# An encoder's front on one core: constant products from the beginning, another order of quarters and casts, a third weight tile, other homes for squares

## The reference, cut to what matters

```
mod = silu(c) @ w_mod + b_mod                     # per sequence: shift1, scale1, gate1, shift2, scale2, gate2
h   = rms_norm(x, g_mix) * (1 + scale1) + shift1  # norm over the 1024 features of a token
z   = h @ w_in                                    # 1024 x 1536: u_f | u_r | u_g
y_f = fourier_mixer(u_f)                          # FFT over sequence and head, real part, a small map per head
u_c = depthwise_conv(u_r)                         # 4 taps along the sequence
y_r = bidirectional_rglru(u_c) * gelu(u_g)        # gates from small products, linear recurrences both ways
x   = x + gate1 * (concat(y_f, y_r) @ w_out)
x   = x + gate2 * (square(relu(h2 @ w_ff1)) @ w_ff2)   # h2: second norm, width 4096 inside
y   = rms_norm(x, g_final)
```

## Time and profile before

| | us |
|---|---|
| median of 3 runs | 1403.32 (1403.24 to 1403.36) |
| profiled execution | 1403.55 |
| its span | 1401.8 |
| TensorE busy | 1379.7 |
| VectorE, ScalarE, GpSimd busy | 812.8, 588.1, 478.0 |

### The profile page before, as it was taken

How to read it: one execution, slowest core, us unless ns; L and a number is a source line. 1 busy time by engine, 2 the same in 40 slices (tenths; PEclk the granted TensorE clock), 3 DMA queues, 4 the chain that set the end, 5 groups by cost and what they waited for, 6 DMA issues and landing times.

```text
span 1401.8 us, 18026 instructions
## 1 busy us (share of the span) xinstructions
PE 1379.7 (98%) x7332; PEld 1170.7 (84%) x7332; DVE 812.8 (58%) x781; ACT 588.1 (42%) x703; POOL 478.0 (34%) x269
## 2 busy tenths in 40 slices
PE   5999999999999999999999999999999999999998
PEld 3877778898888888888888888888888888888887
DVE  5967688795438974555334453353746434354584
ACT  5667888665325632332222222342322223423152
POOL 0002111145003775574554545531432222333131
PEclk9999999999999999999999999999999999999999
DMA  9444411106210343343433334479997444445552
GB/s 368 170 158 158 155 63 38 46 31 215 116 61 31 120 162 124 137 146 140 152 122 114 127 141 152 166 276 388 377 388 285 151 150 155 167 173 197 200 189 90
DMA packets 75699, 231.27 MB, mean 165 GB/s; under 512 B 5729, under 2 KB 9953, under 8 KB 66786
## 3 DMA queue, kind: packets, MB, share of 16 engines
q1 hardware_dynamic: 75074, 229.60, 44.6%
q10 hardware_dynamic: 544, 0.52, 0.1%
HBM read 165.09 MB, written 65.01 MB: 164 GB/s over the span
## 4 chain that ended last, share of the span: by engine, by line
PE 95%; DVE 2%; DMA 1%; SPq 1%; issue 1%; ACT 0%; POOL 0%; DVEq 0%; ACTq 0%
PE bank L827 19%; PE bank L828 19%; PE bank L829 19%; PE bank L821 9%; PE bank L822 9%; PE bank L823 9%; PE bank L837 5%; PE bank L838 3%; DMA mod_first<-in_w_mod 1%; PE bank L866 1%; PE bank L878 0%; DVE two_r L2194 0%; SPq L590 0%; DVE n_t L2166 0%; PE bank L848 0%
## 5 line engine op out<-in xcount | busy, mean ns | idle before, releaser
L2585 POOL TENSOR_TENSOR w_lo<-w_raw,w_hi 128x2048 fp32r<-128x2048 f32 x28 | 134.7, 4812 | 319.6 <-ACT w_hi L1644 318.1
L2312 DVE TENSOR_TENSOR hin_two<-hin,hin_two 128x3072 fp32r<-128x3072 f32 x28 | 130.3, 4657 | 187.7 <-ACT hin_two L1656 187.7
L827 PE MATMUL bank<-hin_two,w_lo 128*128 128x512 f32 (+1 forms) x576 | 211.4, 367 | 0.0
L828 PE MATMUL bank<-hin_two,w_hi 128*128 128x512 f32 (+1 forms) x576 | 210.8, 366 | 0.0
L829 PE MATMUL bank<-hin_two,w_hi 128*128 128x512 f32 (+1 forms) x576 | 210.5, 365 | 0.0
L1644 ACT ACTIVATE w_hi<-w_raw 128x2048 fp32r<-128x2048 f32 x28 | 53.6, 1915 | 247.3 <-PE bank L838 150.2
L2577 POOL TENSOR_TENSOR w_lo<-w_raw,w_hi 128x512 fp32r<-128x512 f32 x43 | 65.4, 1520 | 183.8 <-ACT w_hi L1582 183.7
L827 PEld LDWEIGHTS bank<-hin_two,w_lo 128*128 128x128 f32 x576 | 108.6, 189 | 18.2 <-issue 0.2
L829 PEld LDWEIGHTS bank<-hin_two,w_hi 128*128 128x128 f32 x576 | 108.6, 189 | 17.7
L828 PEld LDWEIGHTS bank<-hin_two,w_hi 128*128 128x128 f32 x576 | 108.7, 189 | 17.0 <-issue 0.2
L1592 ACT ACTIVATE hid<-bank 128x768 f32<-128x768 f32 (+2 forms) x68 | 52.5, 773 | 162.8 <-PE bank L829 152.6
(11 more groups left out here) (297 smaller groups left out, 3473.5 us busy)
## 6 DMA issues: line engine op xcount, KB each, us to landing
hin<-hid_all SPq DMA_DIRECT2D x28, 1536.0 KB, 6.6
hid_all<-hid SPq DMA_DIRECT2D x105, 384.0 KB, 2.5
w_raw<-in_w_ff SPq DMA_DIRECT2D x36, 1024.0 KB, 9.1
mod_raw<-in_w_mod SPq DMA_DIRECT2D x16, 1024.0 KB, 6.0
w_raw<-in_w_ff SPq DMA_DIRECT2D x60, 256.0 KB, 3.2
x<-in_xT SPq DMA_DIRECT2D x5, 2048.0 KB, 14.3
w_sums<-w_raw SPq DMA_DIRECT2D x8, 1024.0 KB, 15.6
w_raw<-w_sums SPq DMA_DIRECT2D x8, 1024.0 KB, 9.7
```

Of the source, the lines that this page charges most:

```text
L827: pe.matmul(out, w_lo, v_hi, start=first, stop=False, skip_group_check=True)
L828: pe.matmul(out, w_hi, v_lo, start=False, stop=False, skip_group_check=True)
L2312: dve.tensor_tensor(hin_part(n % 3, LO), hin[n % 3][:].rearrange("p t n -> p (t n)"), hin_part(n % 3, HI), ALU.subtract).then_inc(hin_lo_d ...
L2585: pool.tensor_tensor(w2_lo[n % 2][:].rearrange("p t n -> p (t n)"), w2_raw[m % RAWS][:].rearrange("p t n -> p (t n)"), w2_hi[n % 2][:].rea ...
```

## The change

- TensorE: instead of 7 products of constants behind `norm_sum(1)`, 44 at the very beginning, ahead of `norm_sum(0)`.
- TensorE: `mod_quarter_sum(0)` comes right behind `mod_quarter(0)`. `front` takes a list of tiles; chunk 0 takes tiles 0, 1 and 2, in pieces; mod_quarter(3) and its sum move between other pieces. Product n = 6 (tile 2, chunk 0) is thereby part of the front; the banks, the order of the copies out (`FRONT`) and `in_tile`'s waits follow.
- ScalarE and VectorE: the row and columns of quarter 0 and the copy of rstd come ahead of the casts of tiles 0 and 1; these come between the first scalings and lo parts. Tile 2 is cast in the front, its lo part on VectorE and no longer on GpSimd.
- Tile 2 has a raw place of its own (`win_raw2`) and is loaded behind quarter 1, ahead of quarter 2.
- Each square has a home of its own, in three sets; chunk 2's lie in chunk 0's x and in the raw place of tile 2, and wait for those to be used up.
- The seven semaphores `op_lo[i]` become one that counts.

```diff
--- before
+++ after
@@ -230,6 +230,7 @@
     win_raw1 = place("win_raw1", [P, KD * P], F32, s2 + 4096)
+    win_raw2 = place("win_raw2", [P, KD * P], F32, W0 + 14336)
@@ -238,8 +239,9 @@
-    sq8 = place("sq8", [P, KD, CH], F32, W0)
-    sq8_other = place("sq8_other", [P, KD, CH], F32, A0 + 32768)
+    sq_at = ([A0 + 81920 + 2048 * k for k in range(KD)], [A0 + 32768 + 2048 * k for k in range(KD)],
+             [X0 + 2048 * k for k in range(4)] + [W0, W0 + 2048, W0 + 4096, W0 + 14336])
+    sq_tile = [[place(f"sq{n}_{k}", [P, CH], F32, o) for k, o in enumerate(homes)] for n, homes in enumerate(sq_at)]
@@ -406,6 +408,7 @@
     ld_x0 = sem("ld_x0_rest")
+    ld_win2 = sem("ld_win2")
@@ -464,7 +467,7 @@
     op_hi = sem("op_hi")
-    op_lo = [sem(f"op_lo{i}") for i in range(7)]
+    op_lo = sem("op_lo")
@@ -507,10 +510,6 @@
-    def squares(n):
-        return sq8_other if n == 1 else sq8
@@ -542,12 +541,16 @@
+    FRONT = (0, 3, 6, 1, 4, 2, 5)
...
     def in_bank(n):
-        return bank[(0, 1, 2, 3, 5, 4)[n] if n < 2 * NCH else n % 4]
+        return bank[(0, 3, 4, 1, 5, 7)[n] if n < 2 * NCH else n % 4]
     def in_order(n):
-        j, c = divmod(n, NCH)
-        return 2 * c + j + 1 if j < 2 else n + 1
+        return FRONT.index(n) + 1 if n in FRONT else n + 1
...
+    def raw_of(j):
+        return {1: win_raw1, 2: win_raw2}.get(j, win_raw)
@@ -601,12 +604,11 @@
         load_first(1)
+        sp.dma_start(win_raw2[:], w_in_d[TILES[2]]).then_inc(ld_win2, 16)
...
         sp.dma_start(dft_head[:], dft_head_d).then_inc(ld_dft, 16)
-        sp.wait_ge(win_lo_done, 1)
-        sp.dma_start(win_raw[:], w_in_d[TILES[2]]).then_inc(ld_win, 16)
@@ -843,7 +845,7 @@
                 pe.wait_ge(xn_done, xn_count(n))
-            total = squares(n)[:, 0, :] if shared(n) else n_acc[:]
+            total = sq_tile[n][0][:] if shared(n) else n_acc[:]
@@ -888,14 +890,13 @@
-        def front(c, q):
+        def front(c, q, tiles=(0, 1)):
             i = part_at[c, q]
-            for j in range(2):
+            for j in tiles:
...
                     pe.wait_ge(win_lo_done, j + 1)
-                    if j == 1:
-                        pe.wait_ge(rstd_copied, c + 1)
+                    pe.wait_ge(rstd_copied, c + 1)
@@ -913,7 +914,7 @@
             n = NCH * j + c
-            pe.wait_ge(in_evac, n - 3)
+            pe.wait_ge(in_evac, {2 * NCH + 1: 2, 2 * NCH + 2: 1, 3 * NCH: 4}.get(n, n - 3))
@@ -935,37 +936,42 @@
         pe.wait_ge(const_set, 4)
+        for b in range(44):
+            pe.matmul(bank[2][:, 0:P], ident[:], ones[:], start=True, stop=True)
...
         mod_quarter(0)
+        mod_quarter_sum(0)
         norm_sum(1)
-        for b in range(7):
-            pe.matmul(bank[2][:, 0:P], ident[:], ones[:], start=True, stop=True)
-        mod_quarter_sum(0)
         norm_spread(1)
+        front(0, 0, (0,))
         mod_quarter(1)
-        front(0, 0)
+        front(0, 0, (1,))
         mod_quarter_sum(1)
+        front(1, 0)
+        front(0, 0, (2,))
         mod_quarter(2)
-        front(1, 0)
+        front(0, 1, (0,))
         mod_quarter_sum(2)
-        front(0, 1)
+        front(0, 1, (1, 2))
         front(1, 1)
+        front(0, 2, (0, 1, 2))
+        norm_sum(2)
         mod_quarter(3)
-        front(0, 2)
+        norm_spread(2)
+        front(1, 2, (0,))
         mod_quarter_sum(3)
-        norm_sum(2)
-        front(1, 2)
-        norm_spread(2)
-        front(0, 3)
+        front(1, 2, (1,))
+        front(0, 3, (0, 1, 2))
         front(1, 3)
+        pe.wait_ge(mod_cols, NQ)
...
             for c in range(NCH):
-                if j > 1:
+                if j > 1 and NCH * j + c not in FRONT:
@@ -1128,7 +1134,7 @@
                 pe.wait_ge(op_hi, hi_count(i, part))
-                pe.wait_ge(op_lo[i], part + 1)
+                pe.wait_ge(op_lo, 7 * part + i + 1)
@@ -1255,9 +1261,11 @@
             if shared(n):
-                if k == 0 and n == 2:
-                    act.wait_ge(norm_mm, 1)
-                dst = squares(n)[:, k, :]
+                if n == 2 and k == 0:
+                    act.wait_ge(hlo_done, 2 * part_at[0, 1] + 2)
+                elif n == 2 and k == KD - 1:
+                    act.wait_ge(win_lo_done, 3)
+                dst = sq_tile[n][k][:]
@@ -1278,13 +1286,12 @@
             else:
-                act.wait_ge(ld_win, 16 * max(j, 1))
-            if j == 2:
-                act.wait_ge(norm_mm, NN)
-            elif j > 2:
-                act.wait_ge(in_mm, NCH * max(2, j - 1))
-            raw = win_raw1 if j == 1 else win_raw
-            act.activation(win_hi[win_of(j)][:].rearrange("p k m -> p (k m)"), raw[:], ACT.Copy
+                act.wait_ge(*((ld_win2, 16) if j == 2 else (ld_win, 16 * max(j - 1, 1))))
+            if j == 3:
+                act.wait_ge(in_mm, len(FRONT))
+            elif j > 3:
+                act.wait_ge(in_mm, NCH * (j - 1))
+            act.activation(win_hi[win_of(j)][:].rearrange("p k m -> p (k m)"), raw_of(j)[:], ACT.Copy
@@ -1325,35 +1332,34 @@
         root(0)
-        square(1, 2)
-        for k in range(3, KD):
+        for k in range(2, KD):
             square(1, k)
+        copy_rstd(0)
+        mod_copy(0)
         split_win_hi(0)
+        root(1)
         split_win_hi(1)
-        root(1)
-        mod_copy(0)
-        copy_rstd(0)
...
         copy_rstd(1)
+        front_hi(1, 0)
         mod_copy(1)
-        front_hi(1, 0)
+        split_win_hi(2)
         front_hi(0, 1)
+        front_hi(1, 1)
         mod_copy(2)
-        front_hi(1, 1)
...
             square(2, k)
-        mod_copy(3)
...
         root(2)
+        mod_copy(3)
+        copy_rstd(2)
...
         front_hi(1, 3)
-        copy_rstd(2)
...
             front_hi(2, q)
-        split_win_hi(2)
@@ -1872,8 +1878,7 @@
             dve.wait_ge(win_hi_done, j + 1)
-            raw = win_raw1 if j == 1 else win_raw
-            dve.tensor_tensor(win_lo[win_of(j)][:].rearrange("p k m -> p (k m)"), raw[:],
+            dve.tensor_tensor(win_lo[win_of(j)][:].rearrange("p k m -> p (k m)"), raw_of(j)[:],
@@ -1898,28 +1903,29 @@
         def add_squares(n, steps=range(KD - 1)):
-            sq = squares(n)
+            sq = sq_tile[n]
...
                     dve.wait_ge(sq_added, adds_v(n) + i)
-                dve.tensor_tensor(sq[:, a, :], sq[:, a, :], sq[:, b, :], ALU.add).then_inc(sq_added, 1)
+                dve.tensor_tensor(sq[a][:], sq[a][:], sq[b][:], ALU.add).then_inc(sq_added, 1)
...
         add_squares(1)
-        split_win_lo(0)
-        split_win_lo(1)
-        rstd(1)
...
         front_scale(0, 0)
+        rstd(1)
+        split_win_lo(0)
         front_lo(0, 0)
+        split_win_lo(1)
...
         front_scale(0, 1)
+        split_win_lo(2)
@@ -1930,9 +1936,9 @@
         front_lo(1, 2)
+        rstd(2)
...
         front_scale(0, 3)
-        rstd(2)
@@ -2191,7 +2197,7 @@
             pair = token_pair(i, part)
-            dve.tensor_tensor(pair[:, LO], token_sums(i, part), pair[:, HI], ALU.subtract).then_inc(op_lo[i], 1)
+            dve.tensor_tensor(pair[:, LO], token_sums(i, part), pair[:, HI], ALU.subtract).then_inc(op_lo, 1)
@@ -2517,8 +2522,7 @@
-        pool.wait_ge(win_lo_done, 2)
-        split_win_lo(2)
+        pool.wait_ge(win_lo_done, 3)
```

More of the change, by code:

```diff
@@ L2509, in split_win_lo @@
             pool.wait_ge(win_hi_done, j + 1)
-            raw = win_raw1 if j == 1 else win_raw
-            pool.tensor_tensor(win_lo[win_of(j)][:].rearrange("p k m -> p (k m)"), raw[:],
+            pool.tensor_tensor(win_lo[win_of(j)][:].rearrange("p k m -> p (k m)"), raw_of(j)[:],
                                win_hi[win_of(j)][:].rearrange("p k m -> p (k m)"), ALU.subtract
```

## The result

| | before | after |
|---|---|---|
| median, us | 1403.38 (1403.24 to 1403.56, 6 runs) | 1411.89 (1410.27 to 1413.37, 6 runs) |
| profiled execution, its span | 1403.55, 1401.8 | 1411.51, 1409.7 |

The ratio is 1.0057, with a 95% interval of 1.0047 to 1.0067: 8.5 us slower, where +4.6 was forecast and the range ended at 1410.8. In the profiled pair the difference is 7.96 us.

What follows compares the result with a forecast made beforehand. TensorE bounds the kernel (busy 1379.7 of 1401.8 us). Shift behind the front −0.7 + 0.6 + 2.7 less 0.1, taken as +2.45, plus convolution wait 2.1, gives +4.6 us: 1407.9 us; 8-in-10 range 1404.8 to 1410.8.

Steps and rivals of the forecast that it cites:

- the first quarter's: Start of the front: quarter 0 handled ahead of the weight casts, first input product at 26.77 instead of 29.45 us.
- Gain up to here: 0.7 us: Up to mod_quarter_sum(1): new order there at 31.6 us, old at 32.3, a gain of 0.7 us.
- one gap of 1.1 us in one run: Argument against the clock falling back: the old order's gap of 1.1 us before 27.59 us didn't lower it.
- Fourth quarter: Front: TensorE waits 2.7 us (bounds 2.2 and 3.2) for VectorE's lo part, asked at 58.44, ready at 61.16 us.
- win_lo(2): Third weight tile's lo part, now on VectorE: ready 35.7 us, asked at 35.26; wait of 0.6 us (bounds 0 and 1.5).
- Convolution: Behind the front: convolution ends at 88.4 us, gate product due at 86.4; new wait 2.1 us (bounds 1.7 and 4.3).
- the rule quoted in the prediction: A VectorE operation with both inputs in SBUF is fully blocked while a GpSimd operation holds their shared port pair.
- The copy decides: Convolution start: chunk 2's u_pad copy, done at 78.3 us, sets it; VectorE's small chain, taken as 4.0 us, ends near 77.8.
- both waits: TensorE's two long new waits: 2.7 us at the fourth quarter and 2.1 us at the gate product behind the convolution.
- rival 1: TensorE's clock falls back to 1.2 GHz between 14.4 and 26.8 us: 1410 to 1411.5 us; chance 0.15.

Runs made afterwards that it cites:

- e12_light: Changed kernel with e4's and e8's edits, 10 wide constant products at the start and shorter wide fillings in five gaps than e9; 1403.64 us, ratio 0.9999.
- e5: Changed kernel with its 44 constant products of 128 columns replaced by 11 of 512 columns; 1411.73 us, ratio 1.0054.
- e1: Changed kernel, 44 products kept, with 18 more constant products in TensorE's gaps between 15.6 and 27 us; 1410.46 us, ratio 1.0047.
- e9: Changed kernel with e4's and e8's edits, wide constant products at the start and constant products in the five gaps; 1404.68 us, ratio 1.0008.
- e11: Changed kernel with only e9's wide constant products at the start and filled gaps; 1410.38 us, ratio 1.0043.
- e2: Kernel before the change with only the 44 constant products added ahead of its first norm sum; 1406.35 us, ratio 1.0017.
- e3: Changed kernel without its 44 constant products; 1411.23 us, ratio 1.0048.
- e4: Changed kernel with mod_quarter(3), its copy, sum and columns put back in their old places; 1410.20 us, ratio 1.0042.
- e6: Changed kernel with VectorE's small chain moved from behind the front to the beginning; 1411.70 us (2 runs).
- e8: Changed kernel with both the small chain at the beginning and chunk 2's tile 0 products ahead of tile 1; 1410.01 us, ratio 1.0044.
- e7: Changed kernel with chunk 2's front products reordered, tile 0 ahead of most of tile 1; 1410.15 us (3 runs).

## Why the prediction was wrong

The step that failed is the first quarter's: "Gain up to here: 0.7 us". It was a loss of 2.0 us. The sum took two things as given: that the clock, once high, stays high (its fall was a rival with a chance of 0.15), and that transfers arrive as in the old order. The stepping itself was sound, as e12_light shows. mod_quarter_sum(1) starts at 31.75 in e12, where neither went wrong; at 33.27 in e5, where the level fell and the packet of instructions was away; and at 34.30 in the changed kernel. So of the 2.7 us between forecast and measurement about 1.5 are the level and 1.0 the later arrivals (0.7 of them there from the first x on), by one profile of each. What the runs showed in place of the step:

- **The level of the clock.** The new order leaves TensorE gaps of 0.7 to 1.6 us up to 27 us, where the old one was full from 22.0 to 26.5 us. The granted clock fell in the profiled run of the changed kernel and of every variant that left the gaps, beginning between 21 and 29 us and for 3.4 to 13.7 us. It fell in e1 too, at 18.7 us, the end of the gap of 1.2 us that its filling left (17.4 to 18.7); in e9, e11 and e12, with no gap over 0.5 us, it did not fall there. With e5 against e11 that makes the gaps the cause. In the changed kernel the fall begins at 24.7 us, in the gap behind `norm_sum(1)`, and that is where the old order had the 7 constant products that the change took away; no run puts them back alone, and in e2 they stood there and the level fell behind the next wait. The prediction's evidence against it, one gap of 1.1 us in one run, was too little: by their mean clock, the slower runs of the kernel before (19 of 64) fell too. The Trainium skill (TensorE: Matmul & The Clock Gate, Part 1) says that the number of slow products at a kernel's start differs from run to run of one kernel. No kernel has two traces here; the scatter of 3 us in the changed kernel, with mean clocks from 0.996 to 0.998, fits it.
- **The instruction packet.** A cause that the prediction did not have. The 44 products are 176 instructions more in TensorE's stream (each makes two records of products and two of weight loads; 148 net of the 7 taken away), and one 16 KB packet of instructions moves from 35 to 38 us to 15 to 21 us, among the transfers that the front waits for. e2, e3 and e5 show that it moves with the number of small products, and what lands next is 1.1 to 1.4 us later where it is early (win_raw 22.58 instead of 21.24 in e2; the second half of mod_quarter(0) 21.15 instead of 19.98 in e4). That it holds up one of the 16 transfer engines is my reading and not shown; its size fits: 6.8% of 16 engines over 1 us is 1.1 us of one engine. What the packet alone costs in time is not shown for the new order, since e5's median did not move. In the changed kernel's own profile 0.7 us of the delay was there already at the first x (its arrival, and all that follows it), which no experiment explains: e1, e2 and e4 don't have it.
- **Fourth quarter.** Right: stepped 2.7, measured 2.5, and e4 takes the wait away entirely.
- **win_lo(2).** Stepped 0.6, measured 0.3.
- **Convolution.** Right in size (2.1 and 1.9), and the hold-up by GpSimd of the earlier trace rows was seen again, at another step, one with a single input tile, to which the rule quoted in the prediction doesn't speak. "The copy decides" was half the truth: the chain took 4.6 us instead of the 4.0 assumed and ended with the copy, and e6 to e8 show two bounds, not one.
- **What I left out of both waits.** Behind a wait of 2 us the level can fall: it did behind the fourth quarter in e5, e6, e8 and e11, and behind the gates in e4. Where it falls, about 1.6 us are added (e5, e6 and e8: 19.5 us instead of 17.9 from the wait to the mod_step). It need not fall: in the profiles of the changed kernel, e1, e3 and e7 it stayed at 1.00 behind both waits. That is a likely reason why taking a wait away saved an amount that single runs don't repeat.

So rival 1 and the forecast both came true. Their sum was given as 1410 to 1411.5; the median is 1411.9, of which the later arrivals, the 0.6 ahead of the mod_step and the 0.5 behind the gates are the rest. The last two stay open.

## What to carry to other kernels

An edit that lets the bounding engine start earlier in pieces is worth only the pieces that touch: gaps of a microsecond in front of dense work can cost more than they give, through the clock, and the cost differs from run to run. Before moving a step past another in a hand-written order, measure how much work of the bounding engine lies between it and its consumer; here 4.5 us became 1.5 for a chain of 4.0. And where two things bound a wait, test them together as well as apart.

## What the runs showed of the hardware

- Constant products in all gaps kept the granted clock at 1.00 through the front (e9, e12) or up to the first long wait (e11); with one gap of 1.2 us left (e1) it fell. Filling that runs over has its price: the first input product at 27.38 us in e9 against 26.85 in e12.
- Instructions are traffic. 44 small products brought a 16 KB packet forward by 15 us or more (from 35 to 38 us to 20 to 21 us in e2); the same columns in 11 products did not.
- One fall of the level costs 1.6 us where it lasts 3.4 us (e5: 63.8 to 67.2 us); the same amount separates the two groups of runs of the kernel before.
